# Recurrent layer of a decoder trunk: the row recursion moves to GpSimd, the weight remainders to VectorE, the decay differences to ScalarE, and the order of the stages is written anew

## The reference

```python
g = jnp.cumsum(g, axis=-1)
diff = g[..., :, None] - g[..., None, :]
decay = jnp.where(causal, jnp.exp(jnp.where(causal, diff, 0.0)), 0.0)
a_mat = jnp.where(strict, jnp.einsum('bhnid,bhnjd->bhnij', k_beta, k) * decay, 0.0)
t_inv = lax.linalg.triangular_solve(a_mat + eye, ...)
v_new = u_n - w_n @ state
out = q_n @ state + intra_n @ v_new
state = state * d_n + k_n.T @ v_new
```

## Time and profile before

| | |
|---|---|
| median of 3 runs | 2259.1 us (2257.13 to 2259.82) |
| the profiled execution | 2258.21 us, span 2256.3 us |
| mean granted TensorE clock | 0.988 |
| busy: PE, DVE, ACT, POOL | 2151.6, 1098.3, 789.8, 269.3 us |
| layer 1's mixer, about | 1424 to 1836 us of the span |

### The profile page before, as it was taken

How to read it: one execution, slowest core, us unless ns; L and a number is a source line. 1 busy time by engine, 2 the same in 40 slices (tenths; PEclk the granted TensorE clock), 3 DMA queues, 4 the chain that set the end, 5 groups by cost and what they waited for, 6 DMA issues and landing times.

```text
span 2256.3 us, 25940 instructions
## 1 busy us (share of the span) xinstructions
PE 2151.6 (95%) x9662; PEld 1714.4 (76%) x9662; DVE 1098.3 (49%) x1827; ACT 789.8 (35%) x1085; POOL 269.3 (12%) x164
## 2 busy tenths in 40 slices
PE   7999999999999999999999999878877899999998
PEld 6888887666667888887888888656766777888886
DVE  4444444687644444423444432466676654444422
ACT  4333223224543333222333322444445444333221
POOL 1000000122211000000000000333333320000001
PEclk9999999999999999999999999989999999999999
DMA  4333322212122333322323332221211222333321
GB/s 168 93 102 93 112 93 67 74 57 65 47 58 92 102 93 94 120 90 78 94 93 97 112 99 83 73 51 38 54 51 48 57 84 89 98 93 101 113 90 51
DMA packets 55965, 190.17 MB, mean 84 GB/s; under 512 B 11728, under 2 KB 11728, under 8 KB 55888
## 3 DMA queue, kind: packets, MB, share of 16 engines
q1 hardware_dynamic: 53680, 189.00, 27.2%
q10 hardware_dynamic: 2208, 0.13, 0.1%
HBM read 186.74 MB, written 2.36 MB: 84 GB/s over the span
## 4 chain that ended last, share of the span: by engine, by line
PE 85%; DVE 8%; ACT 4%; issue 1%; DMA 1%; POOL 0%; SPq 0%; DVEq 0%; ACTq 0%; POOLq 0%
PE prod L431 26%; PE prod L433 25%; PE prod L432 25%; PE misc L633 2%; PE misc L564 1%; DVE rows L1344 1%; PE prod L521 1%; PE misc L582 1%; DVE rows_tmp L1342 1%; DVE vc L1417 1%; ACT w_hi L773 1%; DMA blk<-blocks 1%; DVE rows L1339 1%; PE misc L544 0%; DVE w_lo L1033 0%
## 5 line engine op out<-in xcount | busy, mean ns | idle before, releaser
L431 PE MATMUL prod<-h_hi,w_hi 128*128 128x512 f32 x1856 | 758.8, 409 | 1.8 <-POOL w_lo L1517 1.4
L1033 DVE TENSOR_TENSOR w_lo<-raw,w_hi 128x1024 fp32r<-128x1024 f32 (+1 forms) x267 | 359.4, 1346 | 765.1 <-ACT w_hi L773 764.4
L433 PE MATMUL prod<-h_hi,w_lo 128*128 128x512 f32 x1856 | 726.4, 391 | 0.0
L432 PE MATMUL prod<-h_lo,w_hi 128*128 128x512 f32 x1856 | 725.8, 391 | 0.0
L773 ACT ACTIVATE w_hi<-raw 128x1024 fp32r<-128x1024 f32 (+1 forms) x317 | 356.2, 1124 | 603.6 <-PE prod L433 592.0
L431 PEld LDWEIGHTS prod<-h_hi,w_hi 128*128 128x128 f32 x1856 | 351.0, 189 | 99.9 <-issue 34.5
L433 PEld LDWEIGHTS prod<-h_hi,w_lo 128*128 128x128 f32 x1856 | 350.0, 189 | 74.6
L432 PEld LDWEIGHTS prod<-h_lo,w_hi 128*128 128x128 f32 x1856 | 351.1, 189 | 66.4 <-issue 4.3
L431 PE MATMUL prod<-a_hi,w_hi 128*128 128x512 f32 x704 | 278.1, 395 | 0.0
L433 PE MATMUL prod<-a_hi,w_lo 128*128 128x512 f32 x704 | 278.1, 395 | 0.0
L432 PE MATMUL prod<-a_lo,w_hi 128*128 128x512 f32 x704 | 278.1, 395 | 0.0
(11 more groups left out here) (228 smaller groups left out, 1903.5 us busy)
## 6 DMA issues: line engine op xcount, KB each, us to landing
raw<-in_w SPq DMA_DIRECT2D x253, 512.0 KB, 3.5
raw<-in_wd SPq DMA_DIRECT2D x64, 704.0 KB, 4.1
blk<-blocks SPq DMA_DIRECT2D x8, 512.0 KB
x<-in_x SPq DMA_DIRECT2D x8, 256.0 KB, 5.2
out<-y_out SPq DMA_DIRECT2D x8, 256.0 KB, 2.2
consts<-in_consts SPq DMA_DIRECT2D x1, 768.0 KB, 8.0
blocks<-a_mat SPq DMA_DIRECT2D x40, 4.0 KB, 1.4
raw<-in_w SPq DMA_DIRECT2D x2, 256.0 KB, 4.0
```

The costliest lines, as they stand in the source:

```text
L431: pe.matmul(bank, wh, hi, start=first and k == 0, stop=False)
L432: pe.matmul(bank, wh, lo, start=False, stop=False)
L433: ins = pe.matmul(bank, wl, hi, start=False, stop=last and k == tiles_n - 1)
L1033: dve.tensor_tensor(w_lo[:, n % 2, 0:w], raw[:, n % 4, 0:w], w_hi[:, n % 2, 0:w].bitcast(F32), ALU.subtract).then_inc(lo_ready, 1)
```

## The change

- The row recursion (copy and 15 pairs) is issued by GpSimd as one stage "rows" at slot 3, followed at once by the spread into `t_inv`. The copy that starts it moves behind the lvl masks.
- `w_lo` of layer 1's units goes from GpSimd to VectorE, slot 1 of each unit.
- The two decay differences are eight ScalarE activations with Relu out of PSUM; `dec_t` has two buffers, and `e_last` is a ScalarE copy.
- kk is cut in two: the diagonal (kk, slot 15) and `a_mat` (amat, slot 17).
- decay and mask move 10 and 11 slots forward (from 11 and 13 to 1 and 2), most others move by one or two slots; taps go from slots 3, 4, 6 to 2, 3, 4 and the SiLU from 7 to 5.
- `blk` is loaded with four DMAs in place of one.

```diff
-CHAIN1 = {"spread": -20, "decay": -17, "mask": -15, "kk": -12, "lvl": -8, "qdec": -4, "rows0": -1, "rows1": 0,
-          "rows2": 1, "rows3": 2, "rows4": 3, "rk": -1, "cv": 3, "gram": 5, "tinv": 6, "turn": 9,
-          "y5": 11, "lvl7": 12, "t5": 13, "y6": 15, "t6": 17, "y7": 19, "t7": 21}
+CHAIN1 = {"spread": -30, "decay": -27, "mask": -26, "kk": -13, "amat": -11, "lvl": -10, "qdec": -6, "rows": -1,
+          "rk": -1, "cv": 1, "gram": 3, "turn": 11, "y5": 13, "lvl7": 14, "t5": 15, "y6": 17, "t6": 19, "y7": 21, "t7": 23}
...
+TAP_SLOTS = (2, 3, 4)
+SILU_SLOT = 5
...
@@ SyncE @@
-                        sp.wait_ge(rows_done, g)
-                    sp.dma_start(blk[:].rearrange("p t k j -> p (t k j)"),
+                        sp.wait_ge(t_made, g)
+                    for b in range(0, BLOCKS, 2):
+                        sp.dma_start(blk[b * BLK:(b + 2) * BLK].rearrange("p t k j -> p (t k j)"),
...
@@ ScalarE, decay @@
                     if g >= 1:
                         act.wait_ge(qdec_ready, g)
+                        act.wait_ge(a_made, g)
+                    if g >= 2:
+                        act.wait_ge(gram_used, 2 * (g - 1))
                     act.activation(e_row[:], M[0], ACT.Exp).then_inc(e_row_ready, 1)
+                    for t in range(TT):
+                        act.activation(dec_a[:, t, :], M[0][:, t, :], ACT.Relu, bias=neg_g[:, t, g:g + 1])
+                        ins = act.activation(dec_t[:, i, t, :], M[0][:, t, :], ACT.Relu, bias=g_cum[:, t, g:g + 1],
+                                             scale=-1.0)
+                    ins.then_inc(dif_ready, 1)
...
@@ VectorE @@
-                if name == "decay":
-                    dve.wait_ge(grow_mm, g + 1)
-                    dve.wait_ge(e_row_ready, g + 1)
-                    dve.tensor_copy(e_last[:, g % 3], e_row[:, :, P - 1:P])
...
-                    link(dve.tensor_tensor(dec_a[:], M[0], col(g_cum, g), ALU.subtract))
-                    link(dve.tensor_scalar(dec_t[:], dec_a[:], 0.0, None, ALU.min))
-                    dve.tensor_scalar(dec_a[:], dec_a[:], 0.0, None, ALU.max).then_inc(dif_ready, 1)
...
+                elif k == 1:
+                    split(OD_N + u + 2)
...
@@ GpSimd @@
+                elif name == "rows":
+                    pool.wait_ge(blk_in, 16 * (BLOCKS // 2) * (g + 1))
+                    seq = (2 * BLK - 1) * g + 1
+                    for k in range(BLK - 1, 0, -1):
+                        pool.wait_ge(rows_seq, seq)
+                        pool.tensor_tensor(rows_tmp[:, :, 0:k], blk[:, :, k, 0:k],
+                                           rows[:, :, k:k + 1].broadcast_to([P, TT, k]), ALU.mult).then_inc(rows_seq, 1)
+                        pool.wait_ge(rows_seq, seq + 1)
+                        pool.tensor_tensor(rows[:, :, 0:k], rows[:, :, 0:k], rows_tmp[:, :, 0:k], ALU.subtract)\
+                            .then_inc(rows_seq, 1)
...
-                        pool.tensor_tensor(w_lo[:, n % 2, 0:KT * P], raw[:, n % 4, 0:KT * P],
-                                           w_hi[:, n % 2, 0:KT * P].bitcast(F32), ALU.subtract).then_inc(lo_ready, 1)
```

More of the change, by code:

```diff
@@ L110, in attention_slots @@
     return out
-CHAIN1 = {"spread": -20, "decay": -17, "mask": -15, "kk": -12, "lvl": -8, "qdec": -4, "rows0": -1, "rows1": 0,
-          "rows2": 1, "rows3": 2, "rows4": 3, "rk": -1, "cv": 3, "gram": 5, "tinv": 6, "turn": 9,
-          "y5": 11, "lvl7": 12, "t5": 13, "y6": 15, "t6": 17, "y7": 19, "t7": 21}
[L118 to L121, removed]
+CHAIN1 = {"spread": -30, "decay": -27, "mask": -26, "kk": -13, "amat": -11, "lvl": -10, "qdec": -6, "rows": -1,
+          "rk": -1, "cv": 1, "gram": 3, "turn": 11, "y5": 13, "lvl7": 14, "t5": 15, "y6": 17, "t6": 19, "y7": 21, "t7": 23}
+CHAIN2 = {"new0": 2, "st0": 4, "ks1": 6, "new1": 8, "st1": 10, "ks2": 12, "new2": 14, "st2": 16, "ks3": 18, "new3": 20,
+          "out": 22, "osquare": 23, "osum": 26, "fin": 28}
+SOONEST = {"spread": 10, "decay": 11, "mask": 12}
+TAP_SLOTS = (2, 3, 4)
+SILU_SLOT = 5
 FIRST = 4
@@ L134, in delta_slots @@
             for name, at in chain.items():
-                out.setdefault(per * (g + behind) + FIRST + at, []).append((g, name))
+                slot = max(per * (g + behind) + FIRST + at, SOONEST.get(name, 0))
+                out.setdefault(slot, []).append((g, name))
     for stages in out.values():
@@ L271, in program @@
         state, v_new = od("state", [2, P]), od("v_new", [2, P])
-        g_tok, g_cum = od("g_tok", [TT, HEADS]), od("g_cum", [TT, HEADS])
+        g_tok, g_cum, neg_g = (od(n, [TT, HEADS]) for n in ("g_tok", "g_cum", "neg_g"))
         beta, beg = od("beta", [TT, HEADS]), od("beg", [TT, HEADS])
@@ L941, in stage_act @@
                     act.wait_ge(grow_mm, g + 1)
+                    if g == 0:
+                        act.wait_ge(g_cum_in, 2)
                     if g >= 1:
                         act.wait_ge(qdec_ready, g)
+                        act.wait_ge(a_made, g)
+                    if g >= 2:
+                        act.wait_ge(gram_used, 2 * (g - 1))
                     act.activation(e_row[:], M[0], ACT.Exp).then_inc(e_row_ready, 1)
+                    for t in range(TT):
[3 more added lines that the diff above has]
+                    ins.then_inc(dif_ready, 1)
                 elif name == "mask":
+                    act.wait_ge(e_row_ready, g + 1)
+                    if g >= 3:
+                        act.wait_ge(state_ready, (TT - 1) * (g - 2))
+                    act.activation(e_last[:, g % 3], e_row[:, :, P - 1:P], ACT.Copy)
                     act.wait_ge(dif_ready, g + 1)
-                    act.activation(dec_t[:], dec_t[:], ACT.Exp)
+                    act.activation(dec_t[:, i], dec_t[:, i], ACT.Exp, scale=-1.0)
                     act.activation(dec_a[:], dec_a[:], ACT.Exp, scale=-1.0).then_inc(dec_exp, 1)
@@ L1006, in _ @@
                         act.activation(dst, pre, ACT.Copy, scale=od_conv[:, conv_channel(kind, h), 3:4]).then_inc(tap_done, 1)
-                    if k == 7 and kind in "qkv":
+                    if k == SILU_SLOT and kind in "qkv":
                         act.wait_ge(conv_done, u - 1)
@@ L1333, in stage_dve @@
                     ins.then_inc(a_made, 1)
[L1334 to L1343, removed]
-                        ins = dve.tensor_tensor(rows[:, :, 0:k], rows[:, :, 0:k], rows_tmp[:, :, 0:k], ALU.subtract)
-                        if k > 1:
-                            link(ins)
-                        else:
-                            ins.then_inc(rows_done, 1)
                 elif name == "cv":
@@ L1482, in stage_pool @@
                     pool.wait_ge(dec_exp, g + 1)
-                    pool.tensor_tensor(dec_t[:], dec_t[:], same(const["tri"]), ALU.mult).then_inc(dec_ready, 1)
+                    pool.tensor_tensor(dec_t[:, g % 2], dec_t[:, g % 2], same(const["tri"]), ALU.mult).then_inc(dec_ready, 1)
                 elif name == "lvl":
@@ L1489, in stage_pool @@
                         mask(l)
+                    pool.tensor_copy(rows[:], const["block_eye"][:, 0:BLK].unsqueeze(1).broadcast_to([P, TT, BLK]))\
+                        .then_inc(rows_seq, 1)
                 elif name == "qdec":
@@ L1507, in stage_pool @@
                     mask(LEVELS)
-            pool.wait_ge(lo_ready, OD_N + 2)
-            for u in range(1, len(OD_UNITS) + 1):
-                for k in range(KT):
-                    for g, name in od_slots.get((u - 1) * KT + k, []):
-                        stage_pool(g, name)
-                    if k == 1:
-                        n = OD_N + u + 1
-                        pool.wait_ge(hi_ready, n + 1)
-                        pool.tensor_tensor(w_lo[:, n % 2, 0:KT * P], raw[:, n % 4, 0:KT * P],
-                                           w_hi[:, n % 2, 0:KT * P].bitcast(F32), ALU.subtract).then_inc(lo_ready, 1)
+            for slot in sorted(od_slots):
+                for g, name in od_slots[slot]:
+                    stage_pool(g, name)
             for r in (5, 6):
```

35 lines of the change are left out of this document (18 added, 17 removed).

## The result

The changed kernel takes 2270.5 us (median of 8 runs, 2263.9 to 2271.5) against 2259.5 before: ratio 1.0042, 95% interval 1.003 to 1.0053. It is slower by 0.4%; the forecast was 2235.

What follows compares the result with a forecast made beforehand. TensorE, 85% of the chain, was bound by waits and lost clock. Gains of 7.0 + 5.4 + 5 + 7.5 + 1.4 less 2 gave 24.3 us: 2258.2 to 2233.9 profiled, 2235 as median; range 2208 to 2264.

Steps and rivals of the forecast that it cites:

- The rows, R = 13 us: Row recursion's thirty small operations on GpSimd: 9.9 us with semaphores, plus about 3 us contention with VectorE, a head.
- The rival of the rows as the bound: GpSimd's rows at 0.38 us fixed an operation or more make turn wait 3.1 us or more a head; chance 0.14.
- So rows are hidden up to R = 15.3 us: GpSimd's rows start after the mask at 13.2 us, spread takes 1.3, turn asks at about 29.8: slack of 15.3 us.
- The chain on ScalarE: From `e_row` at 7.15 us through Relus, exponentials, squares and two 1.28 us table loads to v's SiLU, ending at 16.5.
- The wait that it makes: TensorE waits 5.7 us a head by gram, most of it already at osum; 6.3 with hand-overs.
- After it, the other waits of today go: Waits for k's SiLU, the state and v_new on TensorE go; 0.4 us a head left for them.
- One wait of 6 us will do no better: 2.8 us a head: TensorE's granted clock stays below full behind the one long wait, as today, costing 2.8 us a head.
- The ends: Outside the five steady periods: first head gains 5.4 us, first to second 5, seventh to eighth 7.5.
- The four `blk` loads ... hidden: Three more SyncE issues of about 0.6 us, hidden because weights are loaded up to four units ahead.
- 0.14 for slower: Chance that the changed kernel is slower, with GpSimd's rows as the bound.

Runs made afterwards that it cites:

- two kernels without the cover: Four `blk` loads instead of one: changed kernel's operations in the order of before, 2266.0 against 2228.1 us; kernel before, 2292.7 us, 32.8 us slower.
- the rows alone: Kernel before with only the row recursion moved to GpSimd, slots, Relus and `w_lo` as before: 2261.0 us, no difference.
- 2211.5 us kernel: Changed kernel with two `a_mat` buffers, `q_dec` ahead of the lvl masks, one `blk` load and osum's table loaded once: 2211.5 us.
- 2223.3: Changed kernel with two `a_mat` buffers and `q_dec` ahead of the two lvl masks on GpSimd: 2223.3 us, against 2234.6 with two buffers only.

## Why the prediction was wrong

The rows of the changed kernel behind the first three points, GpSimd between the start of the period and the turn on TensorE, then ScalarE:

```profile
1592.23 0.48 PE L433 MATMUL prod<-h_hi,w_hi 128*128 128x512 f32 x1
...
1604.99 0.74 POOL L1500 TENSOR_TENSOR rows_tmp<-blk,rows 128x60 f32<-128x60 f32 x1
1605.81 0.31 POOL L1503 TENSOR_TENSOR rows<-rows,rows_tmp 128x60 f32<-128x60 f32 x1
...
1617.02 0.71 POOL L1503 TENSOR_TENSOR rows<-rows,rows_tmp 128x4 f32<-128x4 f32 x1
1617.81 1.28 POOL L1509 TENSOR_TENSOR t_inv<-rows,consts 128x512 f32<-128x512 f32 x1
...
1619.14 0.65 PE L678 MATMUL misc<-consts,t_inv 128*128 128x128 f32 x4
```

```profile
1643.84 0.60 ACT L952 ACTIVATE e_row<-misc 128x512 f32<-128x512 f32 x1 [2.11 <-issue]
...
1648.60 0.64 ACT L997 ACTIVATE sq<-prod 128x512 f32<-128x512 f32 x1
1649.26 1.28 ACT L971 ACT_TABLE_LOAD   x1
1650.56 0.20 ACT L973 ACTIVATE rk<-rk 128x4 f32<-128x4 f32 x1
...
1652.31 0.63 ACT L1026 ACTIVATE vc<-vc 128x512 f32<-128x512 f32 x1
```

- **The rows, R = 13 us: right.** 12.7 us from 1604.99 to 1617.73, in operations of 0.21 to 0.31 us where VectorE leaves them alone, up to 1.3 where it doesn't. The rival of the rows as the bound did not come.
- **"So rows are hidden up to R = 15.3 us": too large.** The period's slot 0 starts at 1592.23, so the rows begin at 12.8 (forecast 13.2), but the turn starts at 26.9 and not at 29.8. That leaves 12.9 us for rows that take 12.7: the turn starts 0.05 us behind the end of the spread. The rows are hidden with nothing to spare, so rows that start later than that are waited for at the turn.
- **The chain on ScalarE: right.** `e_row` started at 1643.84, behind `q_dec`; no idle time from there to v's SiLU; table loads of 1.28 us with 0.02 behind them (1649.26 to 1650.56), no drain. From `e_row` to the end of the SiLU it took 9.1 us, in the sum about 9.3. **The wait that it makes: too large.** It was 4.1 us at osum and none at gram, against 6.3, because TensorE, slow behind the wait at osum, took 3.6 us from osum to gram (1605.64 to 1609.21) where the sum had 1.7. So about 2 us of the forecast's wait were spent as slow work.
- **"After it, the other waits of today go: k's SiLU stands two slots ahead of kk, the state and v_new follow at once; I leave 0.4 for them": this step failed.** I followed who waits for whom on TensorE, and not what the newly cut diagonal itself waits for. It stands in slot 15 and waits for a mask in slot 18, because of the buffer that it dumps into; ks2's residual is queued behind it, and TensorE waits 2.8 us at new2 in every steady head. Two buffers take 36 us off and give 2234.6. That this is the forecast's 2235 is in part luck: with them the five steady periods gained 17.3 us against before (39.9 us each, forecast 42.0 and a gain of 7.0), and the first and last stretches lost the surplus.
- **"One wait of 6 us will do no better: 2.8 us a head": mis-sized, because there were two waits.** The clock fell behind each, and the mean of the six periods was 0.88. TensorE's busy time was 37.05 a period where the sum had 35.3 (42.0 less the waits of 6.7).
- **The ends.** I had first head 5.4, measured 1.7, of which 1.4 is gram's new place; first to second 5, measured -4.7. Besides new2, TensorE waited there 2.6 for `silu_g` (the spread), 4.89 for `t_inv`, 3.57 and 3.04 for `u_inv`: the first heads' chain is not ahead. The last head lost 6.3 where I had 0; 2.8 of it is place, and 2.61 a wait for `t_inv`. The seventh's 5.7 against 7.5 was nearly right. In the table these ends make up more of the miss than the five periods do.
- **"The four `blk` loads ... hidden": right by cover only.** I priced three issues of 0.6 us, and not the transfers. They cost 38 and 33 us in two kernels without the cover, and 9 in this one.
- **The chances.** 0.14 for slower went to the rows as the bound, a mechanism that occurred with the rows alone (6.3 us a head at the turn) and not in the changed kernel. No rival was that a moved instruction waits for something later in the order, and none that the four transfers themselves take longer.

## What to carry to other kernels

For each stage that is cut or moved, list what it waits for in its new slot, buffers that it only dumps into included, and what is queued behind it on its engine. Look at the granted clock behind each wait: a wait that the change removes can be worth its length and a slow stretch behind it, and one that it makes can cost both. Two costs can hide each other, so repeat an experiment that shows no effect once the other cost is gone. When a DMA is cut in pieces, measure issue to landing again, and look at the outermost dimension of each piece, not only at the number of issues.

## What the runs showed of the hardware

**Four small loads were slower than one of the same bytes.** DMA activity per half microsecond, tenths of 16 engines and GB/s, of the kernel before with four `blk` loads (20 us from 1600):

```profile
DMA  0000121176991101111115999401111000000000
GB/s 0 0 0 16 41 82 57 57 123 246 385 352 57 49 25 57 41 49 57 49 49 188 205 328 303 115 33 49 49 49 49 33 0 0 0 0 0 0 0 0
```

The same bytes in the kernel before, with its one load (20 us from 1629):

```profile
DMA  0002678999754442100004499100000000000000
GB/s 0 0 0 115 213 172 172 262 188 156 131 98 115 147 156 107 49 25 25 0 0 66 123 393 426 41 0 0 0 0 0 0 0 0 0 0 0 0 0 0
```

With four loads long stretches lie between the bursts of the weights at 49 to 57 GB/s, with a busy share of 0.1: one or two of the 16 engines. With one load such a stretch is missing. Each piece has the dimensions `[2, BLK, ...]`, the single load `[BLOCKS, BLK, ...]`. The Trainium skill, "DMA: Bandwidth & Descriptors", Rules for kernel authors, says that an outermost dimension of c < 16, for instance a leading broadcast, confines a transfer to at most c engines. By it each piece would have at most 2, the single load at most 8. The share of 0.1 and the 13.9 against 8.3 us agree with it. No run with another outermost dimension was made, so the rule is supported here, not shown.

**The clock.** Behind the wait of 4.1 us the granted clock was 0.56 from 1604.9 to 1612.0, near the lower of its two levels (1.2 of 2.4 GHz), and 1.00 from 1612.0 to 1627.0; in the longer windows behind the waits of 4.1 and 2.8 us it was 0.76 and 0.81. In the 2211.5 us kernel waits of 2.0 us at osum, 0.8 at gram and 2.0 at the turn left it at 1.00 over six periods. Length alone does not decide: in the kernel before it was 0.50 from 1647.7 to 1650.0, behind a wait of 1.43 us at gram with others of 1.29 and 1.90 ahead of it, TensorE having been busy 3.08 of the 7 us before 1647. Shortening osum's wait from 4.1 to 2.0 was worth more than 2.1 us a head: 11.3 us by five such waits in the kernel with two buffers (2234.6 to 2223.3), though v's SiLU and the turn took 7 us of wait back.
